# Stick-breaking attention: from [key, query] columns with triangular products to [query, key] rows with a running sum

## What is computed

```
z = einsum('bhqd,bhkd->bhqk', qb, kb) * scale
causal = k_pos < q_pos
log_keep = where(causal, -softplus(z), 0.0)
suffix = cumsum(log_keep, axis=3, reverse=True) - log_keep
log_a = log_sigmoid(z) + suffix
a = where(causal, exp(log_a), 0.0)
out = einsum('bhqk,bhkd->bhqd', a, vb)
```

## Time and profile before

| what | us |
|---|---|
| median of 3 runs (1258.36 to 1259.2) | 1259.12 |
| the profiled execution | 1264.33 |
| its span | 1263.0 |
| PE busy in the span | 1194.8 |
| DVE, ACT, POOL busy | 517.6, 557.7, 473.2 |

### The profile page before, as it was taken

The page is one execution under the profiler, slowest core; times in us unless marked ns, Lnnn a source line. Parts: engine busy times, 40 slices in busy tenths (PEclk is TensorE's granted clock), DMA queues, the critical chain, the costliest instruction groups (busy, mean ns, idle before and its releaser), DMA issues.

```text
span 1263.0 us, 15061 instructions
## 1 busy us (share of the span) xinstructions
PE 1194.8 (95%) x5783; PEld 931.7 (74%) x5783; DVE 517.6 (41%) x1092; ACT 557.7 (44%) x1012; POOL 473.2 (37%) x291
## 2 busy tenths in 40 slices
PE   6998998999988999989999999989899999999997
PEld 6776765765766788878676767657788888888886
DVE  4047367466446313335234343341721111644444
ACT  5356466374475563234244444442432222433332
POOL 3344243334243244454122222222544444644441
PEclk9999999999998999999999999987899999999999
DMA  8221121211111233532211112111223333433211
GB/s 237 75 68 51 34 67 34 65 53 31 53 51 34 67 91 93 190 93 61 61 51 51 51 50 68 50 52 50 67 84 100 99 89 96 134 100 99 86 66 67
DMA packets 139801, 95.35 MB, mean 75 GB/s; under 512 B 8801, under 2 KB 124874, under 8 KB 139730
## 3 DMA queue, kind: packets, MB, share of 16 engines
q1 hardware_dynamic: 136112, 89.18, 24.3%
q10 hardware_dynamic: 3618, 5.22, 1.2%
HBM read 91.49 MB, written 2.88 MB: 75 GB/s over the span
## 4 chain that ended last, share of the span: by engine, by line
PE 77%; DVE 13%; ACT 6%; issue 2%; POOL 2%; DMA 1%; SPq 0%; DVEq 0%; ACTq 0%
PE bank L411 21%; PE bank L1166 12%; PE bank L1148 12%; PE bank L440 4%; PE bank L808 4%; PE bank L817 3%; PE bank L946 2%; DVE g L1865 2%; PE bank L833 2%; PE bank L1179 1%; PE bank L958 1%; DVE bank L1910 1%; DVE multipliers L1908 1%; PE bank L631 1%; PE bank L447 1%
## 5 line engine op out<-in xcount | busy, mean ns | idle before, releaser
L2388 POOL TENSOR_TENSOR ring<-raw_ring,ring 128x1024 fp32r<-128x1024 f32 x159 | 386.8, 2437 | 614.0 <-ACT ring L1192 614.0
L411 PE MATMUL bank<-hT,ring 128*128 128x512 f32 x1536 | 410.4, 412 | 3.1 <-POOL ring L2388 2.8
L411 PEld LDWEIGHTS bank<-hT,ring 128*128 128x128 f32 x1536 | 284.9, 194 | 70.8 <-issue 13.9
L1192 ACT CAST ring<-raw_ring 128x1024 fp32r<-128x1024 f32 x160 | 167.0, 1046 | 116.9 <-PE bank L1166 93.8
L1166 PE MATMUL bank<-ring,ring_u 128*128 128x512 f32 x672 | 154.0, 391 | 0.0
L1148 PE MATMUL bank<-hT,ring 128*128 128x512 f32 x672 | 152.5, 389 | 0.0
L1166 PEld LDWEIGHTS bank<-ring,ring_u 128*128 128x128 f32 x672 | 126.2, 188 | 27.6
L1148 PEld LDWEIGHTS bank<-hT,ring 128*128 128x128 f32 x672 | 126.1, 188 | 26.1
L2365 DVE TENSOR_TENSOR ring_u<-u,ring_u 128x1024 fp32r<-128x1024 f32 x32 | 82.4, 2583 | 76.0 <-ACT ring_u L1744 76.0
L2370 DVE TENSOR_TENSOR u<-u 128x512 f32<-128x512 f32 x32 | 22.9, 715 | 139.2 <-ACT u L1751 139.2
L440 PE MATMUL bank<-hT,ring 128*128 128x256 f32 x576 | 70.4, 284 | 2.7 <-DVE hT L1790 2.7
(11 more groups left out here) (297 smaller groups left out, 1614.5 us busy)
## 6 DMA issues: line engine op xcount, KB each, us to landing
raw_ring<-in_w_in SPq DMA_DIRECT2D x144, 256.0 KB, 3.3
raw_ring<-in_w_up SPq DMA_DIRECT2D x64, 256.0 KB, 3.2
raw_ring<-in_w_down SPq DMA_DIRECT2D x64, 256.0 KB, 2.7
raw_ring<-in_w_out SPq DMA_DIRECT2D x32, 256.0 KB, 2.8
x<-in_x SPq DMA_DIRECT2D x4, 512.0 KB, 5.6
raw_ring<-in_w_branch_sb SPq DMA_DIRECT2D x8, 256.0 KB, 2.8
raw_ring<-in_w_branch_gdn SPq DMA_DIRECT2D x8, 256.0 KB, 3.2
x<-in_x ACTq DMA_DIRECT2D x4, 512.0 KB, 5.2
```

The lines of the kernel that those rows point to most:

```text
L411: p = pe.matmul(bank, m.slab_k8(n % 4)[:, a, k, :], m.hT[:, b, k, :], start=term == 0, stop=term == 23)
L1192: act.copy(m.ring[:, q, 0, :], m.raw_ring[:, q, :]).then_inc(s.slab_hi[q], 1)
L2388: pool.tensor_tensor(m.ring[:, q, 1, :], m.raw_ring[:, q, :], m.ring[:, q, 0, :].bitcast(F32), ALU.subtract).then_inc(s.slab_lo[q], 1)
```

## The change

The rows now are [query, key]. Queries of block t_ are on the partitions, the first (t_ + 1) blocks of keys in the columns, w = 128 (t_ + 1), and the order is t_ = 0, 1, 2, 3. Keys and values are stored backwards (ACT writes raw tiles 4 and 5 with a reversed column index), so a sum over later keys is a running sum from the left. stick_log with its triangular products, the masks `negtri`, `negones`, `before`, and POOL's stick_sums are gone. The mask is added in stick_z right after the logits. DVE takes the larger of z and 0, runs a `tensor_tensor_scan` over the row, and subtracts the result from z. ACT takes the exponential. The weights are then transposed on PE (t_ + 1 blocks a head), copied by ACT to SBUF, and used in stick_av, which is now t_ + 1 matmuls of 128 columns a head. The next stick_z waits for that copy. Three semaphores of the delta rule are folded into one, the table of constants has 11 matrices for 14, and the orders of all engines are written anew.

```diff
@@ tensor_program @@
-    def stick_z(i, h, j):
-        ...
-        pe.matmul(bank[:, 0:w], kc[hp, j * P:(j + 1) * P], qc[hp, j * P:T], start=True, stop=True).then_inc(s.sb_z[h], 1)
-    def stick_log(i, h, j):
-        ...
-        pe.matmul(bank[:, 0:P], m.ident_b, m.notbefore_b, start=False, stop=True, skip_group_check=True)
-        p = pe.matmul(bank[:, 0:w], mat["negtri"], L[:, 0:w], start=False, stop=True, skip_group_check=True)
-        if j < 3:
-            p = pe.matmul(bank[:, P:w], mat["negones"], C[:, (j + 1) * P:T], start=False, stop=True, skip_group_check=True)
-    def stick_av(i, h, j):
-        ...
+    def stick_z(i, t_):
+        w = (t_ + 1) * P
+        for h in range(2):
+            hp = slice(64 * h, 64 * h + 64)
+            if t_ == 0:
+                pe.wait_ge(s.sb_qk, 2 * i + 2)
+            if 4 * i + t_:
+                pe.wait_ge(s.sb_w[h], 4 * i + t_)
+            pe.matmul(banks[2 + h][:, 0:w], qc[hp, t_ * P:(t_ + 1) * P], kc[hp, T - w:T], start=True, stop=True)
+        for h in range(2):
+            pe.matmul(banks[2 + h][:, 0:P], m.ident_b, m.ahead_b, start=False, stop=True, skip_group_check=True).then_inc(s.sb_z[h], 1)
+
+    def stick_weights_T(i, h, t_):
+        pe.wait_ge(s.sb_act[h], 16 * i + 4 * t_ + 4)
+        for c in range(t_ + 1):
+            p = pe.transpose(chunk(banks[2 + h], c), chunk((pa, pb)[h], c), ident)
+        p.then_inc(s.sb_wT[h], 1)
+
+    def stick_av(i, t_):
+        if t_ == 0:
             pe.wait_ge(s.sb_v, i + 1)
+        for c in range(t_ + 1):
+            for h in range(2):
+                if c == 0:
+                    pe.wait_ge(s.sb_w[h], 4 * i + t_ + 1)
+                hp, v0 = slice(64 * h, 64 * h + 64), (3 - t_ + c) * P + 64 * h
+                p = pe.matmul(banks[4][hp, t_ * P:(t_ + 1) * P], vn[:, v0:v0 + 64], chunk((Csa, Csb)[h], c), start=c == 0, stop=c == t_, skip_group_check=True)
@@ scalar_program @@
+        dst = m.raw_tiles[n][:, ::-1] if n in (4, 5) else m.raw_tiles[n]
+        act.copy(dst, banks[tile_bank(0, g)]).then_inc(s.tile_a[b], 1)
...
+    def stick_weights(i, t_):
+        w = (t_ + 1) * P
+        for h in range(2):
+            act.wait_ge(s.sb_wT[h], 4 * i + t_ + 1)
+            act.copy((Csa, Csb)[h][:, 0:w], banks[2 + h][:, 0:w]).then_inc(s.sb_w[h], 1)
@@ vector_program @@
-        dve.scalar_tensor_tensor(L[:, 0:w], banks[2 + h][:, 0:w], 0.0, a[:, 0:w], ALU.max, ALU.add).then_inc(s.sb_l[h], 1)
-        dve.tensor_tensor(L[:, 0:P], L[:, 0:P], mat["before"], ALU.mult).then_inc(s.sb_l[h], 1)
+    def stick_soft(i, t_):
+        w = (t_ + 1) * P
+        at = 4 * i + t_
+        for h in range(2):
+            dve.wait_ge(s.sb_act[h], 4 * at + 1)
+            dve.tensor_scalar((La, Lb)[h][:, 0:w], banks[2 + h][:, 0:w], 0.0, None, ALU.max).then_inc(s.sb_l[h], 1)
+        for h in range(2):
+            ...
+            dve.tensor_tensor_scan((Csa, Csb)[h][:, 0:w], (La, Lb)[h][:, 0:w], (pa, pb)[h][:, 0:w], 0.0, ALU.add, ALU.add).then_inc(s.sb_l[h], 1)
+        for h in range(2):
+            dve.wait_ge(s.sb_l[h], 2 * at + 2)
+            dve.tensor_tensor((La, Lb)[h][:, 0:w], banks[2 + h][:, 0:w], (Csa, Csb)[h][:, 0:w], ALU.subtract).then_inc(s.sb_x[h], 1)
@@ gpsimd_program @@
-    def stick_sums(i, h, j):
-        ...
```

More of the change, by code:

```diff
@@ L19 @@
 LAM_INIT = 0.8 - 0.6 * float(np.exp(-0.3 * 0))
-MATS = ["ident", "upper", "after", "negtri", "ones", "negones", "causal", "before", "notbefore", "eye32", "block32"]
+MATS = ["ident", "upper", "after", "ones", "causal", "ahead", "eye32", "block32"]
 BLOCK = 16
@@ L67, in shape_constants @@
     mats = {
-        "ident": p == f, "upper": p <= f, "after": p > f, "negtri": -1.0 * (p >= f),
-        "ones": np.ones((P, P)), "negones": -np.ones((P, P)), "causal": np.where(f > p, NEG, 0.0),
-        "before": p < f, "notbefore": np.where(p >= f, NEG, 0.0),
+        "ident": p == f, "upper": p <= f, "after": p > f, "ones": np.ones((P, P)), "causal": np.where(f > p, NEG, 0.0),
+        "ahead": np.where(P - 1 - f >= p, NEG, 0.0),
         "eye32": p % 32 == f % 32, "block32": p // 32 == f // 32,
@@ L658, in tensor_program @@
[L658 to L674 removed]
+        tiles.to(82)
+        stick_weights_T(i, 0, 0)
+        stick_weights_T(i, 1, 0)
@@ L675, in tensor_program @@
+        tiles.to(85)
+        stick_z(i, 1)
+        stick_av(i, 0)
+        delta_gram(i)
+        tiles.to(110)
+        stick_weights_T(i, 0, 1)
+        stick_weights_T(i, 1, 1)
+        tiles.to(116)
+        stick_z(i, 2)
+        tiles.to(124)
+        stick_av(i, 1)
         delta_level_first(i, 4)
-        tiles.to(122)
-        stick_log(i, 0, 1)
-        stick_log(i, 1, 1)
         delta_level_second(i, 4)
-        stick_z(i, 0, 0)
-        stick_z(i, 1, 0)
-        stick_av(i, 0, 1)
@@ L683, in tensor_program @@
-        stick_av(i, 1, 1)
-        tiles.to(126)
+        tiles.to(133)
+        stick_weights_T(i, 0, 2)
+        stick_weights_T(i, 1, 2)
         delta_level_first(i, 5)
-        tiles.to(130)
-        stick_log(i, 0, 0)
-        stick_log(i, 1, 0)
+        stick_z(i, 3)
+        stick_av(i, 2)
         delta_level_second(i, 5)
-        stick_av(i, 0, 0)
-        stick_av(i, 1, 0)
+        tiles.to(137)
         delta_level_first(i, 6)
-        tiles.to(133)
+        tiles.to(141)
         delta_level_second(i, 6)
-        tiles.to(137)
+        tiles.to(146)
@@ L710, in tensor_program @@
+        tiles.to(159)
         delta_chunk(i, 3)
-        tiles.to(160)
+        tiles.to(167)
         delta_o_sum(i)
@@ L724, in tensor_program @@
     delta_decay(i)
+    tiles.to(12)
+    delta_decay_rows(i)
     tiles.to(20)
-    delta_decay_rows(i)
     stick_v_rows(i)
-    tiles.to(54)
+    tiles.to(48)
     delta_q_sum(i)
-    tiles.to(74)
+    tiles.to(62)
     delta_k_sum(i)
+    tiles.to(71)
     delta_v_rows(i)
@@ L2023, in vector_program @@
         delta_rows(i)
+        least(gate, m.rawg, s.g_sig, 4 * i + 3, s.g_dve)
         delta_substitute(i, 0, 4)
-        stick_soft(i, 0, 2)
-        stick_soft(i, 1, 2)
+        stick_soft(i, 1)
         delta_substitute(i, 4, 15)
```

326 lines of the change are left out of this document (125 added, 201 removed).

## The result

The changed kernel takes 1263.07 us (median of 20 runs, 1261.44 to 1271.51), the kernel before 1260.21 (20 runs, 1258.08 to 1267.25). The ratio is 1.0031, with a 95% interval of 1.002 to 1.0042: slower by 0.3%, where I had forecast 1255.0 and faster. The time itself lies inside my range of 1244 to 1264, at its upper end.

The account below looks back on a forecast made before the run. DVE's chain from gram to the first level and the next slab at the border set floors; PE's work counts in stage 3. Terms 0.9 - 1.2 - 3.8 = -4.1 us from 1259.1 gave 1255.0, range 1244 to 1264.

Parts of the forecast that it names:

- my 1.6: Slow clock behind the q_sum wait: 1.6 us each time, half counted as regained in stages 1 and 2.
- q_sum to gram: Stages 0 to 2: z(0), T(0), z(1), av(0) and 3 more projection matmuls stand ahead of gram, +1.5 us.
- gram to first level: DVE's chain in stages 0 to 2 grows from 19.25 to 19.6 us (19.1 to 20.2), counted as +0.4.
- first level to o_sum: Stages 0 to 2: stick_log goes, transposes, stick_av pieces, projection matmuls and new waits come in; walked through as 1.0 us shorter.
- border, o_sum to q_sum: Stage's end: last tile's copy and DVE's convolutions come earlier, 0.7 us of gain (0 to 1.4).
- stage 3, to the branch: Stage 3, up to the first matmul after the stages: PE's work counts; -4.1, -0.7, about +1.0 of waits: -3.8 us.
- the new waits: First level to o_sum: level 4 second 0.6, T(2) 1.0, z(3) 0.8, solve 1.2, a chunk 0.4 us.
- held-up tensor_tensor: Upper bound for a scan of 512 columns: same-shape tensor_tensor where POOL held it up, 1.75 us; 1.1 was taken.
- The one behind T(1) is hidden by DVE's chain: Clock's slow stretch after PE's wait at T(1), stages 0 to 2, was claimed to cost no time.
- Rival C: Clock falls after the new waits, unhidden: slower, 1269.6 us with all falls, 1262 with half; chance 0.28.
- A: Rival: PE's work decides everywhere and waits stay as they are, -16.4 us, 1242.7; chance 0.10.
- B: Rival: the scan costs what a tensor_tensor does, 1.6 us less in stages 0 to 2, 1 in stage 3, 1249.2; chance 0.17.

Follow-up runs that it names:

- filled kernel before: Kernel before plus idle matmuls in PE's waits (q_sum in stages 1 and 2, first level, two places in stage 3): 1256.46 us, 0.9974.
- filled traces: Traces of two kernels, the one before and the changed one, each with idle matmuls in PE's waits: 1256.46 us and 1269.36 us.
- second trace of before: Kernel before, unchanged, run and profiled once more: 1259.41 us, 0.9986.
- the mask late: Changed kernel with POOL's mask of the last level held back in stages 0 to 2 until DVE finished step 2: 1262.28 us, 1.001.
- gram early: Changed kernel with gram moved on PE ahead of T(0), z(1) and av(0) in stages 0 to 2: 1254.34 us, 0.9958.
- the filled kernel: Changed kernel plus idle matmuls in nearly all of PE's waits, results unused: 1269.36 us, 1.0075, seven runs from 1263.26 to 1274.69.
- the slab early: Changed kernel with the next stage's first slab cast earlier on ACT and split earlier on POOL: alone 1263.34 us, 1.0025; four further kernels build on it.
- T(1)'s wait filled: Changed kernel plus three idle float32 matmuls in PE's wait ahead of T(1), stages 0 to 2: 1263.36 us, 1.0023.

## Why the prediction was wrong

**What held.** PE's busy time fell by 15.4 us (forecast 16), its idle time in the four stages rose from 26.6 to 40.6 us (403.0 - 376.4, 401.0 - 360.4), by 14 where I had 12. T(1) waits 3.34 (3.4), a scan of 512 takes 2.33 / 2 = 1.16 us (1.1), gram to the first level is 19.77 us (19.6), the border waits 1.29 (1.8). T(0) and level 5 in stage 3 wait 3.4 and 3.0 us (4.4 and 3). The mechanism was the forecast's: a chain through DVE bounds stages 0 to 2, and PE's savings go into waits.

**What was luck.** Stage 0 reaches o_sum at 151.0, 1.0 us later than before, where I had 0.9. But its q_sum comes 1.4 us earlier (85.6 against 87.1), since both traces of before have a slow stretch at 52 to 54 (0.50), while that of after and that of the filled kernel before have none (1.00). From q_sum to o_sum stage 0 is 2.4 us longer (65.4 against 63.0), so it missed as the others did.

**What failed.** The medians lie 2.9 us apart and the sum had said 4.1 the other way. So 7 us are to be found. The filled traces have the terms of the sum at the full clock (us; plus is slower):

| term | stages | forecast, each | measured, each |
|---|---|---|---|
| q_sum to gram | 0, 1, 2 | +1.5 | +1.7 (13.65 - 11.98) |
| gram to first level | 0, 1, 2 | +0.4 | +0.5 (19.75 - 19.23) |
| first level to o_sum | 0, 1, 2 | -1.0 | +0.4 (32.11 - 31.74) |
| border, o_sum to q_sum | 1, 2 | -0.7 | -0.5 (23.46 - 23.91) |
| stage 3, to the branch | 3 | -3.8 | -1.4 (estimate, see above) |
| sum | | -2.5 | about +5.3 (5.2 at the branch) |

That is 7.8 us, and the clock gave back a little more than my 1.6. I take the full-clock branch as 467.0 before (468.7 - 1.7) and 472.2 after (473.7 - 1.5). The traces of before reach it 9.8 and 6.3 us after that, the trace of after 2.1. Set to the medians (the second trace of before lies 0.8 above, that of after 0.8 below), the pair is 5.5 and 2.9: 2.6 us in favour of the change. This part rests on single traces.

- **"I walk that stretch through as 1.0 us shorter"** (first level to o_sum) failed most: it is 0.4 longer, 1.4 us a stage in three stages, 4.2 of the 7.8. The number isn't the sum of its own terms. Work written down ahead of it is -5.9 + 1.5 + 0.7 + 0.5 = -3.2, the new waits are 0.6 + 1.0 + 0.8 + 1.2 + 0.4 = +4.0: together +0.8, and +0.2 if the 0.6 us of waits that this stretch had before (0.33 and 0.30) are taken off. The runs show +2.9 of waits (0.46, 1.73, 0.41, 0.77 and 0.16, less the 0.6) and so -2.5 of work. Of the waits only T(2)'s was larger than I had it, 1.73 us for 1.0. Behind it stands the collision of two scans of 384 with POOL's mask, which I had neither placed nor priced; in the run with the mask late T(2) waits 0.96. I had used the held-up tensor_tensor only as an end of the range for the scan. In the period the collision is worth 0.4 us a stage (88.98 - 88.57).
- **Stage 3's -3.8** failed next. I had PE's waits grow by 1.0 us there. They grew by 2.6 (138.30 - 128.73 = 9.6, 136.00 - 123.79 = 12.2). The two that I had listed came out no longer than I said. Not listed were that of q_sum (2.25, 0.7 before) and one of 1.02 us for DVE, behind two scans of 512 that met POOL's split and took 4.50 us instead of 2.33:

```profile
424.34 4.50 DVE L1974 TENSOR_TENSOR_SCAN s<-s,s 128x512 f32<-128x512 f32 x2
...
424.68 3.08 POOL L2369 TENSOR_TENSOR ring<-raw_ring,ring 128x1024 fp32r<-128x1024 f32 x1 [9.46 <-ACT ring L1177]
...
430.77 0.93 PE L412 MATMUL bank<-hT,ring 128*128 128x512 f32 x3 [1.02 <-DVE sig_sb L1853]
```

- **"gram comes 1.5 us later"** and **the border's "0.7 us of gain"** were nearly right. The terms close the period: 1.7 + 0.5 + 0.4 - 0.5 = 2.1, as 89.0 - 86.9.
- **"The one behind T(1) is hidden by DVE's chain"** held. Stages 0 and 2 of the changed kernel have such a stretch, and q_sum to o_sum is 65.39 and 65.42 us there, against 65.51 at the full clock. The one at 210 to 216 in stage 1 lengthens level 4 to level 5 from 8.20 to 9.35 us, and the next level gives 0.85 of it back (5.95 for 6.80): the period is 89.3 for 89.0. So the lower mean clock of the changed kernel (0.967 against 0.974) can't price the change: a part of what it counts is slow stretches in which PE had time to spare.

Rival C was the nearest of the rivals in sign and time, but not in its cause. At the full clock the changed kernel is slower by more than the medians say, filling its waits doesn't make it faster, and filling takes 3 us off the kernel before. Rivals A and B are out: PE's work is no bound (gram early saves 8.7 us without changing it), and the scan has no price of a tensor_tensor.

Open: why the filled kernel has two kinds of executions, and what in the stages decides how the clock runs in the code behind the branch (786 to 788 us of it in most traces, 791 or 790 in three of the five with the slab early, and in these three the window of 780 to 1000 is at 0.91, in all others at 0.92 or 0.93).

## What to carry to other kernels

When a profile shows PE waiting in every period for a chain through other engines, price a change by what it does to that chain: here 15 us of PE work were worth nothing, and moving gram ahead of three small steps and six projection matmuls, with the same work, was worth 8.7 us. When a stretch is walked through, add up the terms that were written down and see that they give the number used. Read a second execution before crediting a slow stretch of the clock to one wait: here two traces of one kernel were 3.5 us apart at the same instruction. Where a new DVE operation reads two tiles in SBUF, look up what POOL has in flight at that moment: an order of issue of 0.03 us decided over 1.1 us of DVE's time, of which 0.4 reached the period.

## What the runs showed of the hardware

- **A scan waits for POOL.** Two scans of 384 took 2.90 us when issued 0.03 us behind a POOL tensor_tensor of 1.28 us and 1.79 to 1.81 without one. The 1.1 us between them are about what was left of POOL's operation (209.08 + 1.28 - 209.11 = 1.25). The Trainium skill (SBUF — State Buffer, Who interferes with whom) says that a DVE instruction with two SBUF inputs contends with a GpSimd instruction that reads SBUF, and that the order of issue decides which of the two is held up. The trace agrees, for a scan. With the scan made a tensor_tensor, the two of 384 were issued 0.04 us behind POOL's mask (206.46 and 206.42) and took 2.12 us.
- **The price of a scan.** Two of 512 columns take 2.33 us and the next instruction starts 2.24 us after them, 1.12 each; a tensor_tensor of the same shape takes 0.68, and 0.60 from start to start (215.49 to 216.09 on the changed kernel's DVE). The Trainium skill (DVE: opcode table, instruction layouts, handler registers and perf-mode slots; Datapath and trigger behaviour) says that the built-in scan runs at half throughput. The trace comes near it: 1.12 us is 1.9 times 0.60.
- **Slow stretches move.** With T(1)'s wait filled from 3.34 to 0.77 us, the clock fell to 0.51 in the same place; with all waits filled it stayed at 1.00 through 160 to 340, and the stage was no shorter. A slow stretch costs the kernel before 1.7 us a period (88.6 against 86.9). In the changed kernel's trace those behind T(1) cost nothing, and the one at 210 to 216 cost 0.3 (89.3 against 89.0). One at 128 to 133, in the filled kernel, did cost its 1.5 us (67.05 against 65.51 from q_sum to o_sum).
